# Four quadrants for both heads, in lock step, in the triangular solve of a linear recurrence; scores of the next pass made inside the pass

## What is computed

```python
def step(state, inp):
    r_t, w_t, k_t, v_t, a_t, b_t = inp
    sa = jnp.einsum('bhvk,bhk->bhv', state, a_t)
    state = state * w_t[:, :, None, :] + sa[..., None] * b_t[:, :, None, :] + v_t[..., None] * k_t[:, :, None, :]
    y = jnp.einsum('bhvk,bhk->bhv', state, r_t)
    return state, y
...
y_f, bonus_f = direction(0)
y_b, bonus_b = direction(1)
y = y_f + y_b
```

## Time and profile before

| | us |
|---|---|
| median of three runs | 2794.49 |
| lowest, highest | 2793.18, 2796.72 |
| profiled execution: span | 2791.3 |
| recurrence, first NT to the end of the last pass | 764 to 1226 |
| PE, DVE, ACT, POOL busy over the span | 2697.6, 1402.7, 1264.0, 1233.6 |

### The profile page before, as it was taken

How to read it: one execution, slowest core, us unless ns; L and a number is a source line. 1 busy time by engine, 2 the same in 40 slices (tenths; PEclk the granted TensorE clock), 3 DMA queues, 4 the chain that set the end, 5 groups by cost and what they waited for, 6 DMA issues and landing times.

```text
span 2791.3 us, 55493 instructions
## 1 busy us (share of the span) xinstructions
PE 2697.6 (97%) x23340; PEld 2154.4 (77%) x23340; DVE 1402.7 (50%) x2503; ACT 1264.0 (45%) x2292; POOL 1233.6 (44%) x1145
## 2 busy tenths in 40 slices
PE   8999999989999999989999999999999999999999
PEld 6678888867778888777888877587777777788887
DVE  6847885055667777754888022612223333244410
ACT  5754443234666666544444235634444453422221
POOL 5234444546733433325444446054443645544443
PEclk9999999999999999999999999999999999999999
DMA  5112332322300000103332322032222322323222
GB/s 177 42 54 91 93 96 91 94 95 91 90 16 6 8 8 8 36 29 98 91 98 87 96 88 76 12 114 74 76 77 69 100 74 91 98 91 98 89 90 78
DMA packets 67079, 208.64 MB, mean 75 GB/s; under 512 B 14736, under 2 KB 15376, under 8 KB 66448
## 3 DMA queue, kind: packets, MB, share of 16 engines
q1 hardware_dynamic: 63680, 192.96, 22.5%
q0 software_dynamic: 2576, 10.78, 1.1%
q10 hardware_dynamic: 576, 1.35, 0.1%
HBM read 199.69 MB, written 4.19 MB: 73 GB/s over the span
## 4 chain that ended last, share of the span: by engine, by line
PE 88%; DVE 6%; ACT 2%; POOL 2%; issue 2%; DMA 0%; SPq 0%; DVEq 0%; ACTq 0%; POOLq 0%
PE banks L1803 22%; PE banks L1805 22%; PE banks L1804 22%; PE banks L826 6%; PE banks L835 1%; PE banks L1975 1%; PE banks L943 1%; POOL low L321 1%; PE banks L819 1%; PE banks L2037 1%; PE banks L2023 1%; PE banks L892 1%; DVE low L550 1%; PE banks L2012 1%; DVE arena L2842 1%
## 5 line engine op out<-in xcount | busy, mean ns | idle before, releaser
L321 POOL TENSOR_TENSOR low<-arena,high 128x256 fp32r<-128x256 f32 (+3 forms) x817 | 967.7, 1207 | 1149.8 <-ACT high L309 1149.7
L1803 PE MATMUL banks<-high,high 128*128 128x512 f32 (+1 forms) x2728 | 1080.8, 396 | 10.9 <-DVE arena L2706 2.9
L1805 PE MATMUL banks<-high,low 128*128 128x512 f32 (+1 forms) x2728 | 1070.5, 392 | 0.0
L1804 PE MATMUL banks<-low,high 128*128 128x512 f32 (+1 forms) x2728 | 1070.1, 392 | 0.0
L309 ACT ACTIVATE high<-arena 128x1024 fp32r<-128x1024 f32 (+1 forms) x376 | 382.1, 1016 | 799.3 <-PE banks L1805 797.7
L1803 PEld LDWEIGHTS banks<-high,high 128*128 128x128 f32 x2728 | 513.5, 188 | 139.2 <-issue 5.5
L1805 PEld LDWEIGHTS banks<-high,low 128*128 128x128 f32 x2728 | 513.4, 188 | 119.6
L1804 PEld LDWEIGHTS banks<-low,high 128*128 128x128 f32 x2728 | 513.7, 188 | 117.8 <-issue 1.9
L2740 DVE TENSOR_TENSOR arena<-banks,arena 128x512 f32<-128x512 f32 x48 | 33.1, 692 | 424.4 <-PE banks L1805 423.3
L2871 DVE SCALAR_TENSOR_TENSOR arena<-arena 128x511 f32<-128x511 f32 x88 | 237.2, 2695 | 3.1
L826 PE MATMUL banks<-arena 64*64 64x64 f32 x5632 | 200.3, 222 | 17.6 <-ACT arena L1204 10.7
(11 more groups left out here) (319 smaller groups left out, 3079.4 us busy)
## 6 DMA issues: line engine op xcount, KB each, us to landing
arena<-weights SPq DMA_DIRECT2D x301, 512.0 KB, 3.5
arena<-weights SPq DMA_DIRECT2D x48, 448.0 KB, 3.3
arena<-weights SPq DMA_DIRECT2D x28, 256.0 KB, 2.6
arena<-tables POOLq DMA_DIRECT2D x5, 448.0 KB, 3.6
arena<-x_t SPq DMA_DIRECT2D x4, 512.0 KB, 5.8
x_spill<-arena POOLq DMA_DIRECT2D x1, 2048.0 KB, 9.4
arena<-x_spill POOLq DMA_DIRECT2D x1, 2048.0 KB, 8.8
out_t<-arena SPq DMA_DIRECT2D x8, 256.0 KB, 4.1
```

The costliest lines, as they stand in the source:

```text
L321: low = pool.tensor_tensor(lo[:, part], ring[w % RING][:, part], hi[:, part].bitcast(F32), ALU.subtract)
L1803: pe.matmul(dst, hi[:, c], x[0], start=kt == 0, stop=False)
L1804: pe.matmul(dst, hi[:, c], x[1], start=False, stop=False)
L1805: mm = pe.matmul(dst, lo[:, c], x[0], start=False, stop=kt == kts_of[t] - 1)
```

## The change

1. `product` and `both_heads` become `both`, which does a product for both heads on all four quadrants. Head 1's matrices of every second step lie in the other half of the partitions. The identity must be added to a power that lies in the right half: a new product `turn_heads` (ID) turns D by a multiplication with the identity, and the powers get the identity added before the product (W2 on POOL, W4 and W8 on DVE) instead of DVE adding the old U behind it, so that U2, U3 and U4 are plain copies by ACT (`grown`).
2. All copies and masks take both heads in one instruction: 128x512 in place of two of 128x256.
3. `turned_scores(i + 1)` and `scores(i + 1)` are made within pass i, before and after U5, for the passes with c = 1, 2, 3 (`early`), into PJ. For c = 0 they stand at the end of the pass before, into PI. The masks of pass i + 1 follow on DVE. AM gets five half buffers in place of two whole ones.
4. `read_state` and `second_state` stand elsewhere, U6 stands behind the state steps, `spread(i, "U5")` now stands before `add_u(5)`.
5. `R.zt` is given up; the channel tile's free half of Y is used.

In PE's program at the head of a pass (c = 2 here), before: L819 is A, L905 the read of the state, L826 a single-head product, L918 and L923 the solve.

The core of the diff:

```diff
+        def both(into, col, lhs, rhs, turned_in):
             for q in range(2):
                 for p in range(2):
                     for h in range(2):
+                        r, to = (hf(p ^ h), hf(p)) if turned_in else (hf(p), hf(p ^ h))
+                        mm = pe.matmul(into[h][to, col + C * q:col + C * q + C], lhs(r, h, q), rhs(r, h, q), start=True, stop=True)
+            return mm
...
         for i in range(ITERS + 1):
             off, seq = i < ITERS, i > 0
             if off:
-                scores(i)
+                square(i, 1)
             if seq:
                 read_state(i - 1, 0)
...
             if off:
+                turn_heads(i)
                 side(i, "masks")
-                square(i, 0, 1)
-                square(i, 1, 1)
+                square(i, 2)
             if seq:
                 solve(i - 1, 0)
             if off:
-                for s in (2, 3):
-                    for h in range(2):
-                        square(i, h, s)
-                        grow(i, h, s)
+                grow(i, 2)
+                square(i, 3)
             if seq:
                 advance_state(i - 1, 0)
-            if off:
-                tokens(i, 0)
-            if seq:
                 second_state(i - 1, 0)
             if off:
-                tokens(i, 1)
-                grow(i, 0, 4)
-                grow(i, 1, 4)
+                grow(i, 3)
+                turn_tokens(i)
+                grow(i, 4)
+                tokens(i)
             if seq:
                 read_state(i - 1, 1)
...
                 side(i, "last sum")
                 merge(i, 1)
+                if early(i + 1):
+                    turned_scores(i + 1)
                 side(i, "merge 1")
-                for h in range(2):
-                    grow(i, h, 5)
+                grow(i, 5)
+                if early(i + 1):
+                    scores(i + 1)
             if seq:
                 solve(i - 1, 1)
             if off:
                 merge(i, 2)
                 side(i, "merge 2")
-                for h in range(2):
-                    grow(i, h, 6)
             if seq:
                 advance_state(i - 1, 1)
                 second_state(i - 1, 1)
+            if off:
+                grow(i, 6)
+                if i + 1 < ITERS and not early(i + 1):
+                    turned_scores(i + 1)
+                    scores(i + 1)
...
+            p2.wait(pool, i, "ID")
+            a2.wait(pool, i, "S1")
             for h in range(2):
-                d2.wait(pool, i, f"D_{h}")
-                g2.inc(pool.tensor_tensor(R.U[i % 2][:, h, :, :], R.D[:, h, :, :],
-                                          eye.unsqueeze(1).to_broadcast([P, 2, C]), ALU.add), f"U1_{h}")
+                w_ = pool.tensor_tensor(R.D[:, h, :, :], R.P2[:, h, 1, :].rearrange("p (q c) -> p q c", q=2),
+                                        eye.unsqueeze(1).to_broadcast([P, 2, C]), ALU.add)
+            g2.inc(w_, "W2")
...
+                p2.wait(dve, i, "ID")
+                with_unit(R.U[i % 2].rearrange("p h q c -> p h (q c)"), both_i[:, :, P:2 * P], "U1")
             if seq:
                 add_values(0)
             if off:
                 spread(i, "M")
-                add_u(2)
+                a2.wait(dve, i, "S2")
+                with_unit(R.P2[:, :, 0, :], R.P4[:, :, 1, :], "W4")
                 spread(i, "U2")
-                add_u(3)
+                p2.wait(dve, i, "S3")
+                with_unit(R.P4[:, :, 0, :], both_j[:, :, 0:P], "W8")
```

More of the change, by code:

```diff
@@ L1230, in act_rwkv @@
             if off:
-                for h in range(2):
-                    ev("S2", h, flat(R.P4[:, h, :, :]), 256)
+                grown(2)
                 if c == 3 and j:
                     rstd(j - 1)
-                for h in range(2):
-                    ev("S3", h, flat(R.D[:, h, :, :]), P)
                 if c == 0 and more:
                     norm_k(j + 1)
-                if c == 3 and more:
-                    factor(j + 1, "ei1")
             if seq:
@@ L1243, in act_rwkv @@
             if off:
-                for h in range(2):
-                    ev("T", h, R.TK[i % 2][:, h, :], 384)
+                grown(3)
+                if c == 3 and more:
+                    factor(j + 1, "ei1")
+                grown(4)
+                ev("T", R.TK[i % 2], both_j[:, :, 0:3 * P])
                 if i == 0:
```

236 lines of the change are left out of this document (135 added, 101 removed).

## The result

| | before | changed |
|---|---|---|
| median | 2795.6 us (four runs beside it) | 2828.79 us |
| lowest, highest | 2793.18, 2797.13 | 2826.57, 2831.02 |
| profiled execution: span | 2791.3 | 2824.7 |
| NT of the first to NT of the last pass | 447.7 | 477.3 |

The changed kernel takes 1.0122 times as long (95% interval 1.0108 to 1.0136), 33 us more. I had forecast 2785, and the range ended at 2806. The recurrence, 764 to 1226 us before, now ends near 1260: the whole difference of the spans lies there.

What follows compares the result with a forecast made beforehand. PE's issue of small products bounds the recurrence. Issue of 11.35 plus waits of 2.86 make 14.2 us a pass against 14.45: 7.7 us less, 2 back for W4, 4 less for outer tiles, say 9.5: 2785.0 us, range 2765 to 2806.

Steps and rivals of the forecast that it cites:

- What bounds the kernel now: Recurrence: PE's issue of small products bounds it, 13.55 us of a 14.45 us pass, with 0.9 us of waits.
- Step 1, four quadrants: Single-head products in the recurrence: four quadrants cut issue by 2.2 us a pass, from 13.55 to 11.35.
- Step 2, the walk of the waits: PE's hand-overs with both heads in lock step: waits of 2.86 us a pass in place of 0.9.
- The largest waits before U5 and M2: PE's waits per tile: 3.05 us for Q1's copy before U5, 2.3 for U5's addition before M2 and early-score masks.
- W4 held, 2 us: W4 on DVE, with both inputs in SBUF: some 0.1 us longer in three of four passes, 2 us back.
- The outer tiles, 4 us less: Tiles 0, 1 and 7 lack part of the side work that the walk waits for: 4 us less.
- The slower rival: W4 on DVE held by POOL's work, 0.6 us in all 32 passes: 17 us more, 2802; with dearer hand-overs, chance 0.17.
- The clock: PE keeps 2.4 GHz; rival: 1.2 GHz in half of the recurrence adds some 180 us, 2965; chance 0.05.
- PE stays the bound, or half of it: Recurrence: all waits beyond 0.9 us a pass covered, 2724, chance 0.06; or half covered, 2755, chance 0.17.

Runs made afterwards that it cites:

- e3: Kernel before the change, with GpSimd's long side work nearly taken away in channel tiles 2 to 7 (k_a on 16 columns, b_k zero-filled): 2788.8 us, ratio 0.9980.
- e2: Changed kernel, with GpSimd's long side work nearly taken away in channel tiles 2 to 7 (k_a on 16 columns, b_k zero-filled): 2801.6 us, ratio 1.0024.
- e7: Changed kernel, with U5's addition put ahead of VectorE's side work in its slot again: 2820.9 us, ratio 1.0096.
- e13: Changed kernel, with TensorE adding the identity for U2 and U3, and U5's addition ahead of VectorE's side work: 2797.5 us, ratio 1.0017.
- e15: Changed kernel, with TensorE adding the identity for U3 in place of W4, and W2 left on GpSimd: 2824.4 us, ratio 1.0118.
- e20: e13 with Q1's copy ahead of a factor on ScalarE in c = 3, and a sigmoid and w2's split moved behind S1's copy: 2793.2 us, ratio 0.9994.
- e8: Changed kernel, with GpSimd's side work in c = 1 to 3 held back until VectorE has done W8: 2856.6 us, ratio 1.0221.
- e14: e13 with ScalarE's two table loads moved away from Q1's copy: 2816.8 us, ratio 1.0089.
- e11: Changed kernel, with TensorE adding the identity for U2 and U3, so W2 and W4 are gone: 2812.8 us, ratio 1.0071.

## Why the prediction was wrong, point by point

- **What bounds the kernel now: right.** PE had little idle time before (27.2 us between the first and the last NT), and the one run that shortened another engine's work in the old kernel gave little (e3, 6 us). Only the 0.9 us of waits a pass that I started from was low: by the starts, gaps were 71.8 us in 31 passes, 2.3 a pass.
- **Step 1, four quadrants: right in rate, high in worth.** `both` is 240 records a pass (7680 in all) at 15 ns. I took 2.2 us a pass from issue, 68 in the 31 passes between the first and the last NT. By the starts of the matmuls, gaps left out, issue there is 375.9 us before and 319.4 after: 56 us less. Half of the missing 12 is my price: in tile 4, at full clock throughout, issue fell from 12.5 to 10.5 us a pass, 2.0 and not 2.2. The other half fits the stretches at 1.2 GHz, but isn't shown to be theirs.
- **Step 2, the walk of the waits: the step that failed.** I had waits grow by 1.96 us a pass, 61 us in 31 passes; the same gaps grew from 71.8 to 157.9, by 86. The walk used DVE's side work at the durations of the earlier trace rows, which were measured while the old kernel's GpSimd met other instructions: there none of the 28 scans and none of the 14 small copies was held. The worst term is W8 ahead of the transposes in c = 3: I had 0.15 us, and in tile 4 PE waited 1.55. In tile 4 the gaps grew from 8.1 to 19.3 us, by 2.8 us a pass. Without GpSimd's long side work (e2) the gaps of all passes are 133.6 us, 62 more than before, close to the 61 that I had walked (though they hold 34 us at 1.2 GHz), and the tile is 57.5, against 56.8. So what failed is the assumption that an instruction of DVE keeps its duration when the order changes; the waits from order and latency came out about right in sum.
- **The largest waits before U5 and M2: half right.** They are there, but the transposes' wait for W8, which I had at 1.85 us a tile, is the largest for DVE. The wait behind U5's addition was real: e7 (7 us) and e13 (15).
- **W4 held, 2 us: mis-sized.** It was held for 0.39 us on average, 12 us in all, and 6.8 of that in tiles 0 and 1. I took the average of L1676, an instruction of 0.29 us at another place; L1550, the other end of my range, was the better guide.
- **The outer tiles, 4 us less: wrong.** Tiles 0 and 1 took 62.3 and 63.9 us, longer than the middle ones, where before they took 57.6 and 57.2 against 57.9; tile 0 had 13.7 us at 1.2 GHz, and W4's two longest holds stand in these tiles.
- **The slower rival: the mechanism right, the place and the price wrong.** I had it as W4 alone, 17 us more, 2802. It is all of DVE's held side work and copies, 21 us by e2 and e3, and W4 replaced by itself changed nothing (e15). With 21 us on my sum it would have been a rival of 2806.
- **The clock: wrong.** I kept 2.4 GHz because the kernel before had held it in seven us with PE busy for 4.73 and no wait would exceed 1.4. It fell nine times, the first time behind 9.5 us with 5.0 of work and a wait of 1.94 us, and also behind 10.8 us with 8.9 of work. One stretch at full clock was no evidence for a whole recurrence.
- **PE stays the bound, or half of it: fell.** DVE's pass with c = 2, which I had named against it, is 16.1 us long with 13.1 of DVE's work.

The miss is 43 us from a forecast of 10 less to 33 more. GpSimd against DVE accounts for 21, the low clock for some 12 (an estimate), the outer tiles' term for 4, and the order of U5's addition for 4 to 15, by the run. By measure the same miss is 12 us less taken from issue and 25 us more put into waits between the first and the last NT. The causes overlap, since a shorter wait also keeps the clock up (e13 has a quarter of the low clock), and no run separates them fully; of these only the 21 are an experiment with its control.

No version beats the kernel before. The best, e20, has the change with six edits (two identity products, U5's addition, Q1's copy, two moves on ScalarE) and takes 0.9994 (0.9985 to 1.0003) times as long: 36 us back from the changed kernel, and level with the old one. Its tile is 56.8 us, the number that I had walked, but by luck: it issues 32 records a pass more than the kernel of the walk and has fewer waits.

## What to carry to other kernels

When a change shortens the bounding engine's work, durations of the other engines that were read before it no longer hold: instructions meet others than before and are held by them, and the wait behind them is now on the path. Before trusting a walk, list which VectorE operations will run beside which GpSimd operations, and price the side work at its held duration wherever a wait comes behind it. Two heads in lock step halve the issue time of their products (30 to 15 ns a record) and leave each copy with nothing of the other head to cover it: the gaps grew from 72 to 158 us, more than the issue fell. So count hand-overs before records.

## What the runs showed of the hardware

- An SBUF copy of 8 columns on VectorE took 171 ns with GpSimd's long work away (e2), 422 beside it in the changed kernel (10 records of 170 to 173 and 4 of 1050) and 1058 in e8, as a mean of 14; GpSimd's own work was stretched less: the three instructions of `k_a` took 3.9 us together, 3.6 before.
- TensorE's clock fell to 1.2 GHz nine times in the changed kernel, behind stretches in which TensorE had work in 5.0 of 9.5 us and up to 8.9 of 10.8 us, with no wait of over 2 us. Two kernels with the same TensorE instructions (e13, e14) spent 10 and 34 us there. A 64x64 record took 225 ns at 2.4 GHz and 314 at 1.2.
- A product of the identity accumulated behind another in the same bank cost about its issue: 7.7 us for the 496 more records of e15 between the first and the last NT, 15 ns each. It took one addition from VectorE (e15), and in e11 one from GpSimd too.
